# Three blocks in one kernel: the raised layers' shift columns split into high and low part, and the bias added on VectorE

## The reference

```python
h = rmsnorm(x, g) * (1 + scale) + shift        # 256 x 1024
proj = h @ w_in                                # second block: 1024 -> 4608
...
f = (rmsnorm(x, g_ffn) * (1 + scale2) + shift2) @ w_ff1    # second block: 1024 -> 4096, then relu squared
...
proj = h @ w_in[l]                             # third block, two layers: 1024 -> 4096
```

## Time and profile before

| | |
|---|---|
| median of 3 runs | 2260.46 us (2253.43 to 2266.82) |
| the profiled execution | 2262.27 us, span 2260.0 us |
| PE busy | 1825.0 us (81%), 14916 matmuls and as many weight loads |
| DVE (VectorE) busy | 787.2 us (35%), 1228 instructions |
| ACT (ScalarE) busy | 525.6 us (23%) |
| POOL busy | 52.3 us (2%) |
| mean granted TensorE clock | 0.784 of full speed |
| DMA | 760.64 MB, mean 337 GB/s |
| raised blocks | 2880 matmuls of 128x258 at L752, 288 at L703 |

### The profile page before, as it was taken

One profiled execution on the slowest core, in us unless ns is written; L12 is line 12 of the kernel. 1 busy time (PEld: TensorE's weight loads), 2 busy tenths in 40 slices (PEclk: granted clock), 3 DMA queues, 4 the chain that ended last, 5 costly groups with the idle time before them and its releaser, 6 DMA issues.

```text
span 2260.0 us, 34009 instructions
## 1 busy us (share of the span) xinstructions
PE 1825.0 (81%) x14916; PEld 1152.0 (51%) x14916; DVE 787.2 (35%) x1228; ACT 525.6 (23%) x857; POOL 52.3 (2%) x85
## 2 busy tenths in 40 slices
PE   5999997777777777677676777767899999999897
PEld 3996752212212222221221222221798999998896
DVE  5656630000000000000000000010775788788777
ACT  2430220000000000000000000000574565365664
POOL 0014000000000000000000000000000000000000
PEclk8999987657757655765765665675999999999999
DMA  9867899999999999999999999999744559853541
GB/s 383 299 229 288 345 393 424 425 425 425 425 426 425 425 426 425 425 426 426 425 425 426 426 425 426 425 425 424 254 146 143 169 164 345 285 172 126 168 131 66
DMA packets 159893, 760.64 MB, mean 337 GB/s; under 512 B 10263, under 2 KB 99095, under 8 KB 108216
## 3 DMA queue, kind: packets, MB, share of 16 engines
q1 hardware_dynamic: 156136, 754.07, 83.6%
q10 hardware_dynamic: 3664, 5.24, 0.7%
HBM read 756.13 MB, written 3.14 MB: 336 GB/s over the span
## 4 chain that ended last, share of the span: by engine, by line
DMA 51%; PE 40%; DVE 6%; ACT 1%; issue 1%; SPq 0%; DVEq 0%; ACTq 0%
DMA arena<-in_w_exp_up 22%; DMA arena<-in_w_exp_gate 22%; PE ps L752 19%; PE ps L1160 4%; DMA ring<-in_w_exp_down 3%; PE ps L1018 3%; PE ps L703 3%; PE ps L1032 2%; DMA ring<-in_w_exp_up 2%; PE ps L653 1%; PE ps L896 1%; DVE ring_lo L1607 1%; PE ps L1142 1%; DVE const L1981 1%; DMA ring<-in_w_in 1%; PE ps L746 1%
## 5 line engine op out<-in xcount | busy, mean ns | idle before, releaser
L1018 PE MATMUL ps<-arena,const 128*32 128x352 f32 x2816 | 407.8, 724 | 163.8 <-DMA arena<-in_w_exp_gate 101.3
L1018 PEld LDWEIGHTS ps<-arena,const 128*32 128x32 f32 x2816 | 99.1, 148 | 460.2 <-DMA arena<-in_w_exp_gate 181.6
L1607 DVE TENSOR_TENSOR ring_lo<-ring,w_hi 128x1024 fp32r<-128x1024 f32 x220 | 267.3, 1218 | 74.0 <-ACT w_hi L1208 73.0
L752 PE MATMUL ps<-u_hi,w_hi 128*128 128x258 f32 x960 | 275.5, 287 | 1.2 <-DVE ring_lo L1607 1.1
L1979 DVE TENSOR_TENSOR tail<-tail,ps 128x704 f32<-128x704 f32 x15 | 13.3, 887 | 743.1 <-PE ps L1018 743.1
L752 PE MATMUL ps<-u_hi,ring_lo 128*128 128x258 f32 x960 | 271.2, 282 | 0.0
L752 PE MATMUL ps<-u_lo,w_hi 128*128 128x258 f32 x960 | 271.0, 282 | 0.0
L1208 ACT ACTIVATE w_hi<-ring 128x1024 fp32r<-128x1024 f32 x220 | 230.2, 1050 | 73.7 <-PE ps L1160 30.5
L1018 PE MATMUL ps<-ring,const 128*32 128x352 f32 x1024 | 159.4, 773 | 49.2 <-DMA ring<-in_w_exp_up 36.7
L752 PEld LDWEIGHTS ps<-u_hi,w_hi 128*128 128x128 f32 x960 | 181.6, 189 | 7.3 <-issue 5.2
L752 PEld LDWEIGHTS ps<-u_lo,w_hi 128*128 128x128 f32 x960 | 181.6, 189 | 0.0
(11 more groups left out here) (279 smaller groups left out, 2358.4 us busy)
## 6 DMA issues: line engine op xcount, KB each, us to landing
arena<-in_w_exp_gate SPq DMA_DIRECT2D x96, 1408.0 KB, 35.3
arena<-in_w_exp_up SPq DMA_DIRECT2D x80, 1408.0 KB, 36.5
ring<-in_w_exp_down SPq DMA_DIRECT2D x64, 1536.0 KB, 38.1
ring<-in_w_exp_up SPq DMA_DIRECT2D x48, 1408.0 KB, 35.3
ring<-in_w_in SPq DMA_DIRECT2D x37, 1536.0 KB, 7.0
ring<-in_w_ada SPq DMA_DIRECT2D x32, 1536.0 KB, 9.5
arena<-in_w_exp_down SPq DMA_DIRECT2D x32, 1536.0 KB, 35.4
ring<-in_w_ff SPq DMA_DIRECT2D x18, 1536.0 KB, 7.3
```

The lines of the kernel that those rows point to most:

```text
L752: m = pe.matmul(ps[:, bank, 0:a.shape[-1]], w, a, start=(k == 0 and j == 0), stop=(k == KD - 1 and j == 2))
L1018: m = pe.matmul(ps[32 * j:32 * j + 32, 2 * (k // 8) + i, 0:FJ // 2], XCUR[:, k % 8, :], SLOT[s][:, at:at + FJ // 2], start=(k % 8 == 0), s ...
L1607: tt(slot(c["u"], KD, c["w"], of=ring_lo)[:, :, at], slot(c["u"], KD, c["w"])[:, :, at], w_hi[:, s % HI, :, :].bitcast(F32), ALU.subtract) ...
```

## The change

`raised_shift` writes two columns of `U_HI` alone: column 256 the shift's high part, column 257 what is left of the shift. The tile `shx`, two of the four instructions and the two ones behind `R` go; `U_LO` is read with 256 columns. `parts` notices that the low input is narrower and then puts the low weights by the high input last, so that the first and the last product have 258 columns and the second 256. Behind a block VectorE multiplies 256 columns by `R` and, in a further instruction of one column, adds columns 256 and 257 and multiplies by 1 or 0.125. Each of the two raises `row_scaled`, and ScalarE waits for both. Tiles keep their 258 columns.

```diff
-        shx = sb("shx", [P, KD, 2])
...
-        R = rs[:, 0:UCOL]
+        R = rs[:, 0:T]
...
             def parts(hi, lo, x_hi, x_lo):
+                if x_hi.shape[-1] > x_lo.shape[-1]:
+                    return (hi, x_hi), (hi, x_lo), (lo, x_hi)
                 return (hi, x_hi), (lo, x_hi), (hi, x_lo)
...
-                return dense_blocks(units, lambda it: (U_HI, U_LO), raise_input(), ready="u_split", each=each)
+                return dense_blocks(units, lambda it: (U_HI, U_LO[:, :, 0:T]), raise_input(), ready="u_split", each=each)
...
-                act.wait_ge(S("row_scaled"), raised[0])
-                at = T if scale == 1.0 else T + 1
+                act.wait_ge(S("row_scaled"), 2 * raised[0])
+                at = T
...
             def raised_shift(shift):
-                link(dve.tensor_copy(shx[:, :, 0:1], shift.unsqueeze(2)))
-                link(ts(shx[:, :, 1:2], shift.unsqueeze(2), 0.125, None, ALU.mult))
-                link(dve.tensor_copy(U_HI[:, :, T:UCOL], shx))
-                link(tt(U_LO[:, :, T:UCOL], shx, U_HI[:, :, T:UCOL].bitcast(F32), ALU.subtract))
+                link(dve.tensor_copy(U_HI[:, :, T:T + 1], shift.unsqueeze(2)))
+                link(tt(U_HI[:, :, T + 1:UCOL], shift.unsqueeze(2), U_HI[:, :, T:T + 1].bitcast(F32), ALU.subtract))
...
-            def scale_rows(it):
+            def scale_rows(it, scale=1.0):
                 waits(*it["done"])
                 waits("evacuated", it["b"] - 2)
-                mark(tt(TMP[:, it["b"] % 3, :], ps[:, it["bank"], 0:UCOL], R, ALU.mult), "row_scaled")
+                a, b = TMP[:, it["b"] % 3, :], ps[:, it["bank"], :]
+                mark(tt(a[:, 0:T], b[:, 0:T], R, ALU.mult), "row_scaled")
+                mark(ts(a[:, T:T + 1], b[:, T:T + 1], b[:, T + 1:UCOL], scale, ALU.add, ALU.mult), "row_scaled")
...
-            link(dve.memset(rs[:, T:UCOL], 1.0))
...
-                            scale_rows(it)
+                            scale_rows(it, 0.125 if it["n"] < 4 else 1.0)
```

## The result

| | before | after |
|---|---|---|
| median of 11 runs | 2260.66 us (2253.43 to 2268.73) | 2270.64 us (2268.34 to 2276.82) |
| the profiled execution | 2262.27 us, span 2260.0 | 2268.34 us, span 2266.0 |

The ratio is 1.0048 [1.0037, 1.0060]: 10.8 us slower (8.4 to 13.6), with 2255.1 forecast and 2267 as the upper end. The profiled execution of after is the fastest of its eleven; its span shows about half of the loss.

What follows compares the result with a forecast made beforehand. TensorE's pace was taken to bound the raised blocks, VectorE the last stretch of an in3 layer. Third product -6.6, instruction +1.6, shift -0.4 made -5.4 us: from 2260.46 to 2255.1 us, range 2247 to 2267.

Steps and rivals of the forecast that it cites:

- The third product: Raised blocks: 992 U_LO products on the path fall from 120.0 to 113.3 ns, -6.6 us (bounds -0.9 to -6.6).
- (a): Third product: two columns gain only 0.9 ns, or only k = 0 becomes cheap; 2260.8 us, together chance 0.27.
- The added instruction: VectorE, one per raised block: 0.18 us each, covered in ff1, 0.10 us at 15 to 16 uncovered places, +1.6 us.
- The shift: raised_shift loses two of four small instructions; only the call before the first out3 layer is on the chain, -0.4 us.
- Order of products: Raised blocks: low input second, low weights third; a weight load still stands before each matmul, cost 0.
- (d): Raised blocks at L752: mixed widths disturb the stream, costing 6.7 ns where it was to be saved; 2268.3 us, chance 0.08.
- (b): Third product gets the higher level of 256 columns, 117.9 ns, so -2.1 us; 2259.6 us, chance 0.15.
- (c): Raised blocks: all three products fall by up to 6.7 ns, -19.8 us; 2241.9 us, chance 0.08.
- A sign of the list: Signs named for a wrong forecast: other block times, a longer in3 end, or a difference before 1598 us.

Runs made afterwards that it cites:

- e2: The kernel before with shx allocated last, behind the arena, and nothing else changed; ratio 1.0047.
- e1: The changed kernel with an unused tile of 64 bytes where shx stood, so later tiles keep their addresses of before; ratio 1.0029 to before.
- e10: e1 measured once more without any edit; ratio 1.0025 to before.
- e11: e1 with the three products in the order of the kernel before; ratio 1.0003 to before.
- e7: The kernel before with all three raised products 256 columns wide, rows still 258 apart, shift left out; 2260.52 us in one execution.
- e8: e7 with the rows of U_HI and U_LO 256 elements apart, shift left out as well; 2248.56 us in one execution.
- e3: e1 with U_LO's rows 256 elements apart instead of 258; ratio 1.0009 to before.
- e6: e3 with U_HI's rows 288 elements apart, so all row starts are at distance 64; ratio 0.9997 to before.
- e5: The kernel before, its three products untouched, with the new one-column VectorE instruction and ScalarE's doubled wait; ratio 1.0019.
- e9: The kernel before measured again without any edit, as a control; ratio 0.9994.
- e14: The kernel before with an unused tile of 128 bytes ahead of tail; 2260.39 us in one execution.
- e15: e6 with the three products in the order of the kernel before; ratio 1.0001 to before.
- e12: e2 with a gap of 64 bytes ahead of all tiles, moving the weights up and the arena back to its address of before; ratio 1.0033.

## Why the prediction was wrong, step by step

**The step that failed: pricing the edits.** The prediction went through added and removed instructions and counted the removal of `shx` as four instructions less two. The tile itself had no term, and it carries the loss: e2 makes that edit alone and reproduces 1.0047 of 1.0048. By paces nearly the same sum: in1 has 864 matmuls on the two tiles, 2.2 ns slower if all had stood at 117.8 (1.9 us), and 6.7 ns for the 624 that stood at 113.3 in the first profile (4.7 us in all); ff2 672 x 5.3 ns = 3.6 us, and 96 x 0.9 ns = 0.1 us for those that stood at 117.8 already; the four output layers 768 x 2.2 ns = 1.7 us. Together 7.3 to 10.1 us, against e2's 10.6 (6.8 to 14.7), if all of it reaches the end of the kernel; of in1's and the first output layer's share no profile shows that. The view that would have warned stood in the prediction: two levels for one shape say that something which is neither width nor clock sets the pace. They were used to bound the third product, and not to ask what moves a stream from one level to another.

**The third product, -6.6 us: measured 0 in after, -1.5 us with the layout of before.** The block gave 0 ns in after and 2880.0 - 2866.7 = 13.3 ns in e1, e10 and e11, 1.7 ns for each of its 8 products; 112 blocks on the path make 1.5 us. The mis-sized number is the 113.3 ns carried over from ff2. The argument was that a 256-column matmul behind a 258-column one costs this wherever ff2 shows it; but a raised row starts 8 bytes further for each k, and e7 and e8 show that the starts are worth as much as the width. Of the rivals (a) comes nearest, with -0.9 and -0.8 us for -1.5, but neither of its forms is shown whole. The first, two columns worth 0.9 ns, is near what e7 gives for the width alone, 26.6 ns from 24 matmuls or 1.1 ns each; what was held against it, 288 cycles falling to 272, would have been 160 ns. The second, that a round start is what makes a product cheap, fails alone: e3 gives U_LO eight round starts and gains nothing on e1; only with U_HI's rows round too (e6) come the 13.4 ns. The lower bound of this term, -0.9 us, was also too sure of a gain: after has none.

**The added instruction, +1.6 us (1.4 to 3.4): 2.5 us by the stretches, 4.3 (1.6 to 7.2) by the medians of e5.** Right in its places (0 in ff1, idle time 0.40 us as forecast, the in3 ends longer by 0.66 and 1.08 us, where over 0.8 had been named as a sign of error for the first) and a little low in its price: 0.21 us against 0.18 for one, and 0.13 to 0.21 us for a place on the path against 0.10.

**The shift, -0.4 us: not visible.** The chain of after leaves VectorE before that point and follows PE (2084.33, 72 matmuls), and so does e5's, which keeps all four instructions.

**Order of products, cost 0:** right where it was made (e1 and e11 have equal raised blocks). In the layout of e6 it was not 0, so it was right for this layout and not as a rule.

**The sum.** Layout +10.6 (6.8 to 14.7), instruction +2.5, third product 0: 13.1 us, where 10.8 (8.4 to 13.6) was measured. With the layout restored: -1.5 + 2.5 = +1.0 for e11, measured +0.7 (-3.2 to +4.5); with ff2's first 672 at the higher level 672 x 4.45 ns = 3.0 more, +4.0 for e1 and e10, measured +6.6 and +5.7, each with some 3 us to either side.

**The other rivals.** (d), whose 2268.3 us lies nearest to the result, has the wrong mechanism: its sign was a block above 2.88 us, and after's is 2.880. (b) and (c) needed blocks of 2.86 and 2.72 us. A sign of the list did show: a difference in the stretch before 1598 us, in in1.

**What stays open.** Which programs have ff2 at 113.33 and which at 117.78 ns at distance 64 (before, e3 to e9 and e11 against e1, e10, e14, e15) repeated for the two programs that were profiled twice, and none of order, row length or gap sorts them. In1's level changes between two executions of one program, and within an execution the level can change at a pause of PE. That 128 bytes is the period rests on e14 alone, whose raised block (2873.3 ns) is not quite before's. And why 64 is fast with 0 and 96 slow is shown as a fact only; no run separates the loading of weights from the reading of the moving operand. No kernel that computes the shift was faster than before by more than its interval: e6 at 0.9997 comes nearest.

## What to carry to other kernels

Removing, adding or resizing a tile moves everything allocated behind it, and that edit needs its own term: give the bytes back with an unused tile, or allocate the tile last, before judging the rest of the change. When a stream that the diff doesn't touch changes its pace (here in1 and ff2), look at addresses first. And a price read from one stream holds for another only if their rows start alike, not merely if they have equal width.

## What the runs showed of the hardware

In this kernel the pace of a 128x256 fp32r matmul with a weight load before each, at a granted clock of 1.00 (the 2.4 GHz level), depends on where the moving operand starts relative to the operand that is loaded; the starts tried are named by their distance modulo 128 bytes. At 64 it is 113.3 or 117.8 ns; at 0 it is 118.7 or 120.0; at 96 it is 118.3 in ff2 and 120.0 in the output layers. The same holds for in1's L746, where the weights move and the input is loaded. A triple then starts every 340.0, 353.3, 356.0 or 360.0 ns, and raised blocks stood at 2880.0, 2866.7, 2853.3, 2840.0 and 2826.7 ns: steps of 13.3 ns, 32 cycles of 2.4 GHz, with e3's 2870.2 and e14's 2873.3 between two of them. e2 and e12 together show the distance at work: same instructions, only the addresses differ.

The Trainium skill, SBUF — State Buffer, section "Who interferes with whom", gives TensorE two independent read ports, one for the moving operand and one for the weight load, and says that TensorE waits for no other engine; TensorE: Matmul & The Clock Gate, section "Step-by-step: what each phase is for", says that loading the next weights takes no bandwidth from the running matmul. By these before and e2 would have equal paces. They have 113.33 and 118.67 ns in ff2, so the measurement decides: in this kernel the two are not free of each other, or of the address. And by "Back-to-back issue gap" on the same page the gap of an isolated matmul of 256 columns is 109.2 ns; no stream of the dense layers of any run here reached it.
